# Second layer of a hybrid decoder step: sample states made and turned inside the output product, four tiles normalised earlier

## What is computed

```python
s = (s * jnp.exp(lw_t)[:, :, None, :]
     - s_kk[..., :, None] * (kk_t * a_t)[..., None, :]
     + v_t[..., :, None] * k_t[..., None, :])
...
mean = jnp.mean(o, axis=-1, keepdims=True)
var = jnp.mean(jnp.square(o - mean), axis=-1, keepdims=True)
on = ((o - mean) * lax.rsqrt(var + GN_EPS)).reshape(bsz, t_len, D_MODEL) * ln_w + ln_b
bonus = jnp.sum(heads(r) * heads(k) * r_k, axis=-1, keepdims=True) * heads(v)
on = on + bonus.reshape(bsz, t_len, D_MODEL)
return (on.astype(xn.dtype) * g) @ w_o, s_new, xn[:, -1], v_first
```

## Time and profile before

| | |
|---|---|
| time before, median of 3 runs | 1948.87 us (1943.2 to 1954.48) |
| the profiled execution: its time | 1946.39 us |
| its span in the profile | 1944.2 us |
| PE busy | 1780.6 us, 92% of the span |
| DVE busy | 1027.1 us, 53% |
| ACT busy | 768.8 us, 40% |
| POOL busy | 142.0 us, 7% |
| mean granted TensorE clock | 0.934 of full speed |

### The profile page before, as it was taken

One profiled execution on the slowest core, in us unless ns is written; L12 is line 12 of the kernel. 1 busy time (PEld: TensorE's weight loads), 2 busy tenths in 40 slices (PEclk: granted clock), 3 DMA queues, 4 the chain that ended last, 5 costly groups with the idle time before them and its releaser, 6 DMA issues.

```text
span 1944.2 us, 43041 instructions
## 1 busy us (share of the span) xinstructions
PE 1780.6 (92%) x18633; PEld 1677.4 (86%) x18633; DVE 1027.1 (53%) x1486; ACT 768.8 (40%) x1027; POOL 142.0 (7%) x178
## 2 busy tenths in 40 slices
PE   7999878899999999989998877777799999999997
PEld 6999875899999999987886767765499999999997
DVE  4476765544433444455887546643834442444444
ACT  4353354354412223334455235542436541222343
POOL 1042550000000000300000000001110000000000
PEclk8999989899999999999999858887899999999999
DMA  4322241333332233420221200010043232233321
GB/s 128 87 66 55 55 110 31 98 109 88 101 93 65 86 90 91 116 67 23 76 66 55 67 3 4 4 26 24 12 114 109 86 103 82 71 89 94 93 66 58
DMA packets 235550, 139.05 MB, mean 72 GB/s; under 512 B 4688, under 2 KB 230352, under 8 KB 235408
## 3 DMA queue, kind: packets, MB, share of 16 engines
q1 hardware_dynamic: 227824, 117.25, 20.9%
q0 software_dynamic: 4704, 15.46, 3.2%
q10 hardware_dynamic: 2880, 4.21, 0.6%
HBM read 128.74 MB, written 8.16 MB: 70 GB/s over the span
## 4 chain that ended last, share of the span: by engine, by line
PE 79%; DVE 10%; ACT 5%; issue 3%; POOL 1%; DMA 1%; ACTq 0%; SPq 0%; DVEq 0%; POOLq 0%
PE ps L343 62%; PE ps L2312 2%; PE ps L2306 1%; PE ps L1601 1%; ACT w_head L307 1%; DVE w_rest L312 1%; PE ps L1835 1%; PE ps L2321 1%; POOL mix L957 1%; PE ps L1066 1%; PE ps L1853 1%; PE ps L1142 1%; DVE x_split L2003 1%; PE ps L1872 1%; PE ps L2588 1%
## 5 line engine op out<-in xcount | busy, mean ns | idle before, releaser
L343 PE MATMUL ps<-x_split,w_head 128*128 128x272 f32 (+1 forms) x5472 | 928.7, 292 | 32.2 <-DVE x_split L2003 10.5
L343 PEld LDWEIGHTS ps<-x_split,w_head 128*128 128x128 f32 x5472 | 786.2, 191 | 52.4 <-issue 34.8
L343 PE MATMUL ps<-x_split,w_rest 128*128 128x272 f32 (+2 forms) x2736 | 572.3, 291 | 0.0
L307 ACT ACTIVATE w_head<-w_raw 128x1024 fp32r<-128x1024 f32 (+1 forms) x206 | 228.2, 1108 | 593.6 <-PE ps L343 576.2
L343 PEld LDWEIGHTS ps<-x_split,w_rest 128*128 128x128 f32 x2736 | 434.2, 192 | 0.0
L312 DVE TENSOR_TENSOR w_rest<-w_raw,w_head 128x1024 fp32r<-128x1024 f32 (+1 forms) x206 | 268.5, 1303 | 183.8 <-ACT w_head L307 183.7
L343 PE MATMUL ps<-hidden_split,w_head 128*128 128x272 f32 x1408 | 233.2, 287 | 0.0
L343 PEld LDWEIGHTS ps<-hidden_split,w_head 128*128 128x128 f32 x1408 | 198.0, 188 | 0.0
L343 PE MATMUL ps<-hidden_split,w_rest 128*128 128x272 f32 x704 | 145.3, 287 | 0.0
L1432 DVE TENSOR_TENSOR hT<-hT,ps 128x544 f32<-128x544 f32 (+1 forms) x40 | 28.9, 721 | 161.1 <-PE ps L343 161.1
L343 PEld LDWEIGHTS ps<-hidden_split,w_rest 128*128 128x128 f32 x704 | 110.1, 188 | 0.0
(11 more groups left out here) (446 smaller groups left out, 2070.8 us busy)
## 6 DMA issues: line engine op xcount, KB each, us to landing
w_raw<-in_w_ffn_gate SPq DMA_DIRECT2D x44, 512.0 KB, 3.7
w_raw<-in_w_ffn_up SPq DMA_DIRECT2D x44, 512.0 KB, 3.7
w_raw<-in_w_ffn_down SPq DMA_DIRECT2D x32, 704.0 KB, 4.7
w_raw<-in_w_in_even SPq DMA_DIRECT2D x29, 512.0 KB, 3.8
w_raw<-in_w_ple_gate SPq DMA_DIRECT2D x16, 512.0 KB, 4.0
w_raw<-in_w_out_even SPq DMA_DIRECT2D x8, 512.0 KB, 4.1
w_raw<-in_rw_wr SPq DMA_DIRECT2D x8, 512.0 KB, 4.1
w_raw<-in_rw_wk SPq DMA_DIRECT2D x8, 512.0 KB, 4.0
```

The lines of the kernel that those rows point to most:

```text
L307: act.activation(wh[:, s, 0:kt * P], raw[:, s, 0:kt * P], ACT.Copy).then_inc(head_ok[s], 1)
L343: mm = pe.matmul(ps[:, 2 * s + h, 0:half.stop - half.start], w[:, s, k * P:(k + 1) * P], x[:, k, half], start=first and k == 0, stop=k == ...
```

## The change

What it does:
- The masked values use two buffers in `mix` in place of four in the space of `x_split`. The second may be written only after the last bonus product (`bonus7`), and masking k waits for the state product before it.
- The four state products on PE leave the late stage and stand in the middle of output units 0 to 3; DVE's two `new_state` of each follow the unit's weight rest. ACT's wait for the last of them ahead of tile 0's head is gone.
- The nine states are turned in the middle of units 4 to 7: two, two, three, two. None is turned in unit 0 or units 1 to 3.
- Scale and shift of tiles 0 to 3 move into the late stage: tile 0 after step 7, tile 1 after step 8, tiles 2 and 3 after step 9 (a function `late_normal`). The loop over tiles does them only from tile 4 on.

```diff
-        vux2 = [quad[:, 2048 + 512 * k:2560 + 512 * k] for k in range(4)]
+        vux2 = [mix[:, 23392:23904], mix[:, 24832:25344]]
...
             for k in range(KT):
-                if k >= 4:
-                    pool.wait_ge(*O2.pe.at(f"ns{k // 2 - 2}"))
-                pool.tensor_tensor(vux2[k % 4].rearrange("p (b v) -> p b v", b=NB),
+                if k >= 2:
+                    pool.wait_ge(*O2.pe.at(f"ns{k // 2 - 1}"))
+                elif k == 1:
+                    pool.wait_ge(*O3.pe.at(f"bonus{KT - 1}"))
+                pool.tensor_tensor(vux2[k % 2].rearrange("p (b v) -> p b v", b=NB),
...
-                if q in (2, 4, 6, 8):
-                    pe_new_states(pe, (q - 2) // 2)
...
-            act.wait_ge(*O2.pe.at("ns3"))
...
-                if i in (2, 4, 6):
-                    act_state_rows(act, i // 2 - 1)
...
-                if q in (2, 4, 6, 8):
-                    new_state(dve, q - 2)
-                    new_state(dve, q - 1)
+                for i in {7: (0,), 8: (1,), 9: (2, 3)}.get(q, ()):
+                    late_normal(dve, i)
...
+                if i >= 4:
+                    late_normal(dve, i)
...
+        def late_normal(dve, i):
+            x = values_of(i)
+            by_pairs = x.rearrange("p (k t) -> p k t", k=KT)
+            dve.wait_ge(*O3.act.at(f"rs{i // 4 * 4}"))
+            dve.scalar_tensor_tensor(out=x, in0=x, scalar=col("rw_lnw", i), in1=factors_of(i), op0=ALU.mult,
+                                     op1=ALU.mult).then_inc(*O3.dve.done(f"n{i}"))
+            dve.wait_ge(*O3.dve.at(f"n{i}"))
+            dve.wait_ge(*O3.dve.at(f"bo{i}"))
+            dve.scalar_tensor_tensor(out=by_pairs, in0=by_pairs, scalar=col("rw_lnb", i), in1=v_of(i), op0=ALU.add,
+                                     op1=ALU.add).then_inc(*O3.dve.done(f"on{i}"))
...
-            if k in (2, 4, 6):
-                pe_state_rows(pe, k // 2 - 1)
...
+        rows_in = {4: (0, 1), 5: (2, 3), 6: (4, 5, 6), 7: (7, 8)}
+
+        def states_between(pe, u):
+            if u < 4:
+                pe_new_states(pe, u)
+            for b in rows_in.get(u, ()):
+                pe_state_rows(pe, b)
...
-                between = (lambda: pe_state_rows(pe, u + 2)) if 1 <= u < KT - 1 else None
-                unit_products(pe, "rw_o", u // 2, u % 2, o_ready if u == 0 else None, between=between)
+                unit_products(pe, "rw_o", u // 2, u % 2, o_ready if u == 0 else None, between=lambda: states_between(pe, u))
...
-                if 1 <= u < KT - 1:
-                    act_state_rows(act, u + 2)
+                for b in rows_in.get(u, ()):
+                    act_state_rows(act, b)
...
                 ahead(dve_rest, dve, "rw_o", s, i, u >= KT - 2)
+                if u < 4:
+                    new_state(dve, 2 * u)
+                    new_state(dve, 2 * u + 1)
                 add_squares(dve, norm_f1, s, u)
```

More of the change, by code:

```diff
@@ L2690, in pe_new_states @@
                     mm = pe.matmul(ps[64 * c:64 * c + 64, new_bank(p), :], kb_sample[r, i, c, :],
-                                   vux2[(2 * i + g) % 4][r, :], start=True, stop=True)
+                                   vux2[g][r, :], start=True, stop=True)
             mm.then_inc(*O2.pe.done(f"ns{i}"))
```

## The result

| | before | changed |
|---|---|---|
| median of 20 runs | 1947.47 us (1940.64 to 1954.48) | 1957.82 us (1952.0 to 1982.0) |
| ratio of the runs, 95% interval | | 1.0067 (1.0047 to 1.0087) |
| the profiled execution: time, span | 1946.39, 1944.2 us | 1957.03, 1955.1 us |

The changed kernel is 0.67% slower, about 13 us by the ratio and 10 by the medians; the ratio goes by means, in which two runs near 1980 us weigh. The slowest run, 1982.0 us, was in a slower state of the chip and is not in the ratio. A second set of seven runs gave 1956.43 us and 1.0047 (1.0030 to 1.0065). The profile's span grew by 10.9 us.

A forecast was written before the change was run, and what follows sets the result against it. PE was taken to bound the output units without gaps, a chain around the engines the late stage, DVE being fullest in the tile loop; -9 + 18.9 + 3.3 = +13.2 us on 1946.4 made 1959.6, predicted as 1959.5, range 1948 to 1967.

The forecast's parts named there:

- Output units, +18.9: Output units: added turned states and state products, plus PE's waits for ACT and DVE, cost 18.9 us; ends 17 and 21.
- Late stage, 7.1 gained: First state product to last bonus reading: 31.0 us become 23.9, 7.1 gained; at least 5 if half clock stays.
- ACT's pause: Late stage: PE waits 3.0 us while ACT's table loads, exponentials, squares and logarithm run.
- Tile loop, 1.3 gained and raised to 1.9: Tile loop: early normalisation and moved state work gain 1.3 us; with the late stage 8.4, taken as 9.
- the term for POOL: Unit 0: two maskings on POOL beside DVE's scaling cost 0.2 us each, 0.4 in all.
- Half clock: Tile loop: PE taken at half clock, so 0.2 us saved in each of six rounds, 1.2 in all.
- going from 8.4 to 9: First two stages: gain raised from 8.4 to 9 us, as DVE has tiles 4 to 7 scaled before PE asks.
- The clock, +3.3: Units 4 and 6, about as thin as an earlier low-clock stretch: two stretches of 1.65 us, 3.3; ends 0 and 6.6.
- Full clock in the first stages: Rival 1, 25%: clock stays 1.00 in late stage and tile loop, gain 15 us, kernel at 1952.
- What is removed counts in full: Rival 2, 6%: all work removed from the first stages' chain counts, -24.4 + 18.9 = -5.5 us, kernel at 1941.
- The clock stays low in the units: Rival 3, 13%: clock stays low through units with pauses, 8.9 us above the forecast, kernel at 1968.5.
- Nothing to see: Rival 4, 6%: PE's waits in the units lie beside work on the path anyway; some 1948 us.

The follow-up runs named there:

- e0: The changed kernel again, unaltered: 1956.43 us, ratio 1.0047 to the kernel before; units 66.00 us.
- e4: Changed kernel with scale and shift of tiles 0 to 3 back in the tile loop: 1962.22 us beside 1949.39, ratio 1.0062 to the kernel before.
- e6: Changed kernel, but maskings 2 and later also wait for the last tile's rest on DVE: ratio 1.0044 to the kernel before.
- a1: Another profile of the changed kernel, unaltered: units 66.03 us at clock 1.00.
- e3: Changed kernel with state products after k = 6 and turned states three tiles apart: 1946.8 us beside 1947.52, ratio 0.9996 to the kernel before.
- b1: Second profile of the kernel before, unaltered; b1 and b2 took 35.55 and 36.97 us from first to last bonus reading.
- b2: Third profile of the kernel before, unaltered; b1 and b2 took 35.55 and 36.97 us from first to last bonus reading.
- e1: Changed kernel with turned states of one unit two tiles apart: 1951.48 us, ratio 1.0020 to the kernel before.
- e7: As e4, but ACT takes all exponentials after the last logarithm, none at step 6: 1960.35 us, ratio 1.0064 to the kernel before.
- e2: Changed kernel with state products and the first turning after k = 6 in place of k = 4: 1952.35 us, ratio 1.0021 to the kernel before.

## Why the prediction was right, point by point

The forecast was 1959.5 us, slower; it became 1957.82, slower by 0.67%.

- **Output units, +18.9: measured +18.7** in the pair of profiles, and 66.0 us again in e0, e4, e6 and a1. The units took 8.7 (1 to 3), 10.6, 9.1, 11.2 and 9.1 us, where I had 8.6, 10.8, 9.2, 11.5 and 9.2. The parts hold too. The five waits for ACT come to 6.9 us in the view of waits; taking them away gave 6.4 (predicted 6.7). The four for DVE come to 6.4; taking them away gave 5.9 (predicted 6.5). The rest is the work, 6.3 in e3 (predicted 5.7). The point that decided was the earlier trace rows: in a stretch where PE has no gap, the distance between PE's arrival (3.45 us after the addition) and DVE's last state (5.1) is paid in full.
- **Late stage, 7.1 gained: 7.0** between the same instructions. Over ten profiles it is rather 5.6, as the clock decides (b1, b2, a1). The term was right for the executions compared; over many, the lower end of its range, 5, is as near as the value taken. ACT's pause, put at 3.0 us, is 3.06. The parts behind the pause fit less well than the sum: the last two sums and bonuses took 5.1 us (1369.54 to 1374.62, the clock at 0.50 from 1372 on) where I had 4.1, and the 1.3 for the last reading behind tile 1's normalisation was 0.7, since DVE had finished that and waited 1.02 us for PE. The two errors have opposite signs and cancel in part, which is luck. The reading of the stage was also one-sided: the chain through DVE was there, but PE, called not full, idled only 5.0 of its 33.0 us, so taking the chain away could earn little beyond the moved work.
- **Tile loop, 1.3 gained and raised to 1.9: 0.9.** The samples' result came at 1380.7, where I had 3.1 us more behind the reading, and that part holds: 5.6 from the reading's start against 2.4. The miss is the term for POOL: 0.4 predicted, 1.4 measured (e6 gives 1.6 back). The step that failed was to price the conflict by L2721, which had met POOL for only part of its time. Another meeting was not in the sum at all: the second masking ran at 1374.67 and tile 2's scaling, at 1375.23, took 1.03 us in place of 0.75.
The Trainium skill (SBUF — State Buffer, "Who interferes with whom") has the loser wait for the whole of the other instruction; an estimate from that rule and the 1.04 us of a masking is up to 2.1 us for this pair. The trace lies between: DVE's two took 2.94 and POOL's two 2.96 us, where alone they take 1.50 and 2.05. From POOL's start to DVE's end are 3.50 us, so the four nearly ran one after the other (3.55), which is the rule's picture.
Two more steps failed. Half clock was taken for the loop, but it ended early: the clock was 0.50 from 1376 to 1384 and 1.00 from 1386 on. And the reason for going from 8.4 to 9, that DVE would have tiles 4 to 7 scaled before PE asks, did not hold: DVE's scaling of each of them stands in the chain of waits.

```profile
1376.00:1378.00 2.00, 1.01 (x3) 0.29 (x1) 1.93 (x4) 1.39 (x1) 0.00 (x0) 0.50 0.00 0
...
1386.00:1388.00 2.00, 1.97 (x13) 1.49 (x12) 1.97 (x3) 0.66 (x1) 0.00 (x0) 1.00 0.00 0
```

```profile
1387.35 0.67 DVE mix L2886
1388.05 0.76 DVE mix L2890
```

Tiles 2 and 3 took rounds of 1.28 and 2.27 us in place of 2.81, the next three 2.81 as before; I had 0.2 saved in each of six. From the reading's start on, the loop took 28.23, 28.19 and 27.42 us in the three profiles of the kernel before and 27.33, 27.42, 27.44 and 29.53 (e1) in the four with the changed code, so over many executions no gain is shown here.
- **The clock, +3.3: measured 0.** The step that failed was "about as thin": the earlier trace rows with PE busy 1.89 of 3.80 us lost the clock, and unit 4 with 2.11 of 4.60 kept it. e7 shows that it can fall either way from one execution to another: the same pauses cost 1.57 us there, close to the 1.65 that I had for one stretch. The price was right and its number too high: one stretch in six profiles of these units (the two of the changed kernel, e4, e6, e7 and a1).
- **The sum.** -9 + 18.9 + 3.3 = +13.2 predicted; -7.9 + 18.7 + 0 = +10.8 in the profiles. The error in the clock term and that in the first two stages had opposite signs. With the averages over more profiles, 5.6 for the late stage, nothing for the loop, 18.7 and one low stretch in six, it is some +13.4, so that the nearness of the sum is in part luck, while the term that decided, the units, is not.
- **The rivals.** Full clock in the first stages (1) did not come: 0.83 and 0.82. "What is removed counts in full" (2) is refuted by the late stage's rows: PE's own work fills it but for 3.06 us. "The clock stays low in the units" (3) holds for no profile; the three runs near 1980 us have its sign (a low mean clock) and lie more than 20 us above the median where it had 9 above the forecast, but no trace of such a run exists, so whether that is their cause stays open. (Its 8.9 should be 9.1: twice 8 x 0.78, less 3.3.) "Nothing to see" (4) fell with e1 and e2.

## What to carry to other kernels

Work taken from a stage with gaps and put into one without must bring its own distance: look up when the engine without gaps arrives, when the other engines are ready, and put the work behind the later of the two (here k = 6 in place of k = 4, and turned states three tiles apart, worth 12.4 us). Even then it only broke even, since most of what the late stage gained (4.7 of 6.7 us in the first pair of profiles) was PE's own work, which has to be paid in the units again. Before taking a chain out of a stage, look at how long the engine that does the most there is really idle. Compare profiles stage by stage between fixed instructions, since one stage's clock can move it by 8 us from one execution to the next.

## What was not expected of the hardware

- The same late stage took 26.3 to 34.6 us as its mean granted clock went from 0.87 to 0.65; PE's idle time in it was 3.05 to 3.07 us each time.
- Equal pauses (2.1 us of work in 4.6) left the clock at 1.00 in one execution and brought it down in another, for 1.57 us.
- A VectorE operation with two SBUF inputs took 1.53 us beside a GpSimd multiplication and 0.75 without; POOL's took 1.48 in place of 1.03.
